# Cross attention's scores of all four units computed at once into four banks, and the router's chain reordered around the count

## The reference

```python
h = h + y @ w_out[layer]                       # after the three mixers
h = h + cross_attention(rms_norm(h, norm_cross[layer]), rms_norm(mem, norm_mem[layer]),
                        x_w_q[layer], x_w_kv[layer], x_q_norm[layer], x_k_norm[layer], x_w_o[layer])
hn = rms_norm(h, norm_ffn[layer])
# layer 0: dense SwiGLU. layer 1: top-2-of-8 experts
...
# cross_attention: 4 heads of 64, 256 memory tokens, QK-norm
s = jnp.einsum('bshd,bmhd->bhsm', q, k).astype(jnp.float32) * HEAD_DIM ** -0.5
p = jax.nn.softmax(s, axis=-1).astype(v.dtype)
o = jnp.einsum('bhsm,bmhd->bshd', p, v).reshape(bsz, seq, X_WIDTH)
...
# moe_swiglu
logits = (x2 @ w_router).astype(jnp.float32)
top_val, top_idx = lax.top_k(logits, TOP_K)
gate = jax.nn.softmax(top_val, axis=-1)
# each token goes through its two experts, weighted by gate
```

## Time and profile before

| | us |
|---|---|
| median of 3 runs | 1373.01 |
| lowest, highest of them | 1373.0, 1373.81 |
| the profiled execution's own time | 1374.09 |
| span of its trace | 1372.3 |
| TensorE busy | 1310.5 (96%) |
| VectorE busy | 636.4 (46%) |
| ScalarE busy | 425.5 (31%) |
| GpSimd busy | 89.8 (7%) |
| granted TensorE clock, mean | 0.976 |
| HBM read | 355.88 MB, 260 GB/s over the span |

### The profile page before, as it was taken

The page is one execution under the profiler, slowest core; times in us unless marked ns, Lnnn a source line. Parts: engine busy times, 40 slices in busy tenths (PEclk is TensorE's granted clock), DMA queues, the critical chain, the costliest instruction groups (busy, mean ns, idle before and its releaser), DMA issues.

```text
span 1372.3 us, 48306 instructions
## 1 busy us (share of the span) xinstructions
PE 1310.5 (96%) x21428; PEld 1079.5 (79%) x21428; DVE 636.4 (46%) x1404; ACT 425.5 (31%) x847; POOL 89.8 (7%) x139
## 2 busy tenths in 40 slices
PE   7998897999999999989789999999999999999998
PEld 5855555777777685554659999999999999999997
DVE  7876313103322237651245555555555555455554
ACT  4425413001002122541313333343333333333332
POOL 0450100000000017000100000000000000000000
PEclk9997899999999999999889999999999999999999
DMA  8530043244241054102649999999999999999990
GB/s 351 211 123 1 1 184 122 90 171 184 104 172 62 34 240 154 63 1 90 248 175 390 426 426 427 426 427 426 426 426 427 427 426 426 427 426 426 426 403 33
DMA packets 32865, 357.68 MB, mean 261 GB/s; under 512 B 3715, under 2 KB 5379, under 8 KB 6700
## 3 DMA queue, kind: packets, MB, share of 16 engines
q1 hardware_dynamic: 30656, 353.78, 62.4%
q10 hardware_dynamic: 2156, 3.18, 0.7%
HBM read 355.88 MB, written 1.06 MB: 260 GB/s over the span
## 4 chain that ended last, share of the span: by engine, by line
PE 88%; DVE 5%; ACT 3%; issue 2%; DMA 1%; POOL 1%; ACTq 0%; POOLq 0%; DVEq 0%
PE bank L2102 29%; PE bank L1556 26%; PE bank L2118 14%; PE bank L2049 6%; PE bank L2164 2%; PE bank L2089 2%; PE bank L1564 1%; PE bank L1829 1%; PE bank L1706 1%; PE bank L1576 1%; PE bank L1894 1%; ACT ring L575 1%; DVE ring L968 1%; PE bank L1650 1%; PE bank L2002 0%
## 5 line engine op out<-in xcount | busy, mean ns | idle before, releaser
L2102 PE MATMUL bank<-R,ring 128*64 128x80 f32 x11264 | 421.7, 233 | 0.7 <-DVEq L950 0.7
L2102 PEld LDWEIGHTS bank<-R,ring 128*64 128x64 f32 x11264 | 403.0, 137 | 8.3 <-issue 8.3
L1556 PE MATMUL bank<-ring 128*128 128x256 f32 (+1 forms) x1408 | 368.4, 421 | 8.6 <-DVE ring L968 4.9
L1556 PEld LDWEIGHTS bank<-ring 128*128 128x128 f32 x1408 | 269.4, 193 | 106.2 <-issue 67.3
L841 ACT ACTIVATE ring<-ring 128x1024 f32<-128x1024 f32 x176 | 186.0, 1057 | 146.7 <-PE bank L2118 146.7
L2118 PE MATMUL bank<-zz,ring 128*64 128x80 f32 x5632 | 224.8, 233 | 0.0
L2118 PEld LDWEIGHTS bank<-zz,ring 128*64 128x64 f32 x5632 | 207.9, 137 | 0.0
L1518 DVE SCALAR_TENSOR_TENSOR zz<-zz,bank 128x80 f32<-128x80 f32 x176 | 41.9, 238 | 198.8 <-PE bank L2102 198.3
L1497 DVE COPY ring<-ring 128x1024 f32<-128x1024 f32 x177 | 121.6, 687 | 1.9 <-DVE R L1487 1.9
L1501 DVE COPY ring<-ring 128x1024 f32<-128x1024 f32 x177 | 121.5, 686 | 0.1
L837 ACT ACTIVATE X<-bank 128x80 f32<-128x80 f32 x176 | 41.7, 237 | 246.1 <-PE bank L2102 246.1
(11 more groups left out here) (299 smaller groups left out, 1029.4 us busy)
## 6 DMA issues: line engine op xcount, KB each, us to landing
ring<-moe_w_dram SPq DMA_DIRECT2D x177, 1536.0 KB, 10.7
ring<-ffn_w_dram SPq DMA_DIRECT2D x11, 3072.0 KB, 10.2
ring<-w_in_dram SPq DMA_DIRECT2D x6, 2048.0 KB, 10.4
ring<-w_out_dram SPq DMA_DIRECT2D x4, 2048.0 KB, 8.5
ring<-w_x_dram SPq DMA_DIRECT2D x2, 3072.0 KB, 10.6
ring<-w_small_dram SPq DMA_DIRECT2D x2, 2896.0 KB, 10.1
ring<-w_in_dram SPq DMA_DIRECT2D x2, 2144.0 KB, 21.0
ring<-bias_rows_dram ACTq DMA_DIRECT2D x1, 1536.0 KB, 11.1
```

Of the source, the lines that this page charges most:

```text
L1556: i = pe.matmul(out_ap, a, b, start=(k == 0), stop=(k == n - 1))
L2102: e = pe.matmul(pb[out_bank][c0:c0 + 64, 0:CAP], half[:, P * k + c0:P * k + c0 + 64], xg[:, k], start=(k == 0), stop=(k == KT - 1), tile_p ...
```

## The change

In cross attention, `xscores(0)` and `xscores(1)` stand next to each other ahead of the loop over the units, and the four units' scores have a bank each (6, 7, 4, 3). `nmx` is used with a place of its own for each unit (`nmx` had four already, for the attention before), so the maxima wait only for the last exponentials of the attention before. In the router, the clearing of `table` and `zeros` stands in front of the wait for the logits, the gate half of the table and the first step of `pos` in front of the wait for the count, and the overflow flag with its signals behind `pick(0)`.

```diff
@@ -44,6 +44,7 @@
 HEADS = [0, 4, 1, 5, 2, 6, 3, 7]
 SLOTS = 4
 BU_BANKS = [3, 4, 7, 1, 3, 4, 7, 3]
+XS_BANKS = [6, 7, 4, 3]
 S5_AT = [dict(bu0=4, bu4=7, bu6=9, ys0=10), dict(bu0=3, bu4=6, bu6=9, ys0=9)]
 UPW, DNW = KT * 2 * 256, 2 * D
 FF_SLOTS = [2, 3, 1, 0, 2, 3, 1, 0, 2, 3, 1]
@@ -213,7 +214,7 @@
             a(f"cross_T{g}_", g % 2)
         a("xq", 2, 2); a("xqT_", 3)
         for u in range(4):
-            a(f"xs{u}_", 6 + u % 2, 0)
+            a(f"xs{u}_", XS_BANKS[u], 0)
             a(f"xpT{u}_", u % 2)
         a("xo0_", 2); a("xo1_", 5); a("xoT", 3)
         for g in range(4):
@@ -570,10 +571,10 @@
                 act.activation(R[:, 0], turn_rows, ACT.Sin,
                                scale=-2 * math.pi, bias=cst[:, C_Q:C_Q + 1]).then_inc(sem["angles_ready"], 1)
 
-            def probs(buf, b, src, scale, to):
+            def probs(buf, b, src, scale, to, m):
 
                 return act.activation(s_of[buf][:, b * src.shape[-1]:(b + 1) * src.shape[-1]], src, ACT.Exp,
-                                      bias=nmx[:, buf, b:b + 1], scale=scale, accum_out=to)
+                                      bias=nmx[:, m, b:b + 1], scale=scale, accum_out=to)
 
             def pt_copy(buf, freed, name, n):
 
@@ -737,7 +738,7 @@
                     if v < 2 * NH:
                         act.wait_ge(sem["max_ready"], u + 1)
                         for b in range(2):
-                            e = probs(at(v), b, s_of[at(v)][:, b * nk:b * nk + nk], 1.0, sums[:, i, b, hh:hh + 1])
+                            e = probs(at(v), b, s_of[at(v)][:, b * nk:b * nk + nk], 1.0, sums[:, i, b, hh:hh + 1], at(v))
                         e.then_inc(sem["probs_ready"], 1)
                     if v == 1:
                         cmp_tanh()
@@ -802,7 +803,7 @@
                         banks.wait(act, f"xpT{k - 2}_{l}" if k >= 2 else f"pT1{NH - 2 + k}_{l}")
                         for b in range(2):
                             e = probs(k % 2, b, ps(f"xs{k}_{l}")[:, 256 * b:256 * b + 256], SCALE,
-                                      sums[:, i, 0, 2 * b + hp:2 * b + hp + 1])
+                                      sums[:, i, 0, 2 * b + hp:2 * b + hp + 1], k)
                         e.then_inc(sem["probs_ready"], 1)
                     if k:
                         pt_copy((k - 1) % 2, u - 2, f"xpT{k - 1}_{l}", 512)
@@ -1395,9 +1396,9 @@
                 for k in range(4):
                     u = 20 * l + 16 + k
                     banks.wait(dve, f"xs{k}_{l}")
-                    dve.wait_ge(sem["probs_ready"], u - 1)
-                    own(dve.tensor_reduce(nmx[:, u % 2], ps(f"xs{k}_{l}")[:].rearrange("p (b s) -> p b s", b=2), AX, ALU.max, negate=True))
-                    dve.tensor_scalar(nmx[:, u % 2], nmx[:, u % 2], SCALE, None, ALU.mult).then_inc(sem["max_ready"], 1)
+                    dve.wait_ge(sem["probs_ready"], 20 * l + 16)
+                    own(dve.tensor_reduce(nmx[:, k], ps(f"xs{k}_{l}")[:].rearrange("p (b s) -> p b s", b=2), AX, ALU.max, negate=True))
+                    dve.tensor_scalar(nmx[:, k], nmx[:, k], SCALE, None, ALU.mult).then_inc(sem["max_ready"], 1)
                 for i in range(NT):
                     dve.wait_ge(sem["probs_ready"], 20 * l + 18 + 2 * i)
                     own(dve.reciprocal(sumc[:, i, 0, 0:4], sums[:, i, 0, 0:4]))
@@ -1432,8 +1433,10 @@
                         dve.scalar_tensor_tensor(hT[:, t % 2], hT[:, 2 + t % 2], 0.5, up[:, 256:512], ALU.mult, ALU.mult).then_inc(sem["gated"], 1)
                     add_in("down")
 
+            own(dve.memset(table, 0.0))
+            own(dve.memset(zeros, 0.0))
+            dve.wait_ge(sem["moe_consts_loaded"], 16)
             banks.wait(dve, "router")
-            dve.wait_ge(sem["moe_consts_loaded"], 16)
             own(dve.tensor_copy(lg, ps("router")[:, 0:16].rearrange("p (i e) -> p i e", i=NT)))
             of_j = lg.unsqueeze(2).to_broadcast([P, NT, E, E])
             of_e = lg.unsqueeze(3).to_broadcast([P, NT, E, E])
@@ -1452,20 +1455,24 @@
             own(dve.tensor_reduce(gsum[:, 0:2], ex, AX, ALU.add))
             own(dve.reciprocal(gsum[:, 0:2], gsum[:, 0:2]))
             own(dve.tensor_tensor(ex, ex, spread(gsum[:, 0:2], [P, NT, E]), ALU.mult))
+            for i in range(NT):
+                own(dve.tensor_copy(table[:, 0:PASSES * E, 2 + i].rearrange("p (q e) -> p q e", e=E),
+                                    ex[:, i].unsqueeze(1).to_broadcast([P, PASSES, E])))
+            own(dve.tensor_scalar(pos, sel, -1e4, 1e4, ALU.mult, ALU.add))
 
             banks.wait(dve, "count")
-            own(dve.tensor_scalar(pos, sel, -1e4, 1e4, ALU.mult, ALU.add))
             own(dve.tensor_tensor(pos, pos, ps("count")[:, 0:16].rearrange("p (i e) -> p i e", i=NT), ALU.add))
-            own(dve.memset(table, 0.0))
+            passes = cste[:, C_PASS - C_MOE:C_PASS - C_MOE + PASSES * E].rearrange("p (q e) -> p q e", e=E)
             for i in range(NT):
-                own(dve.tensor_tensor(table[:, 0:PASSES * E, i].rearrange("p (q e) -> p q e", e=E), pos[:, i].unsqueeze(1).to_broadcast([P, PASSES, E]),
-                                      cste[:, C_PASS - C_MOE:C_PASS - C_MOE + PASSES * E].rearrange("p (q e) -> p q e", e=E), ALU.subtract))
-                own(dve.tensor_copy(table[:, 0:PASSES * E, 2 + i].rearrange("p (q e) -> p q e", e=E), ex[:, i].unsqueeze(1).to_broadcast([P, PASSES, E])))
-            own(dve.tensor_reduce(mx2[:, 2:3], ps("count")[:, 16:24], AX, ALU.max))
-            own(dve.tensor_scalar(flag[:, 0:1], mx2[0:1, 2:3], CAP + 0.5, None, ALU.is_gt))
-            signal(banks.drain("count"))
-            signal(banks.drain("router"))
-            signal(sem["flag_ready"])
+                own(dve.tensor_tensor(table[:, 0:PASSES * E, i].rearrange("p (q e) -> p q e", e=E),
+                                      pos[:, i].unsqueeze(1).to_broadcast([P, PASSES, E]), passes, ALU.subtract))
+
+            def overflow():
+                own(dve.tensor_reduce(mx2[:, 2:3], ps("count")[:, 16:24], AX, ALU.max))
+                own(dve.tensor_scalar(flag[:, 0:1], mx2[0:1, 2:3], CAP + 0.5, None, ALU.is_gt))
+                signal(banks.drain("count"))
+                signal(banks.drain("router"))
+                signal(sem["flag_ready"])
 
             def pick(e, wait_to):
 
@@ -1500,8 +1507,8 @@
                 expert_in(dve, turn, t)
                 dve.tensor_copy(st_value, hs[:, HS_ORDER[t % NHS], 1024:2048]).then_inc(sem["value_staged"], 1)
 
-            dve.memset(zeros, 0.0)
             pick(0, lambda k: dve.wait_ge(sem["e_step"], 1))
+            overflow()
             stage_gate(0, 0)
             for g in range(2):
                 gather_half("", g)
@@ -1993,6 +2000,7 @@
                 drained(f"mkT_{l}")
                 drained(f"xqT_{l}")
                 xscores(0)
+                xscores(1)
                 for k in range(4):
                     u = 20 * l + 16 + k
                     nm = f"xpT{k}_{l}"
@@ -2003,8 +2011,6 @@
                         if l == L - 1 and k == 2 and c == 0:
                             e.then_inc(sem["late0_read"], 1)
                     done(nm, e)
-                    if k == 1:
-                        xscores(1)
                     if k:
                         xvalues(k - 1)
                 xvalues(3)
```

## The result

| | before | changed |
|---|---|---|
| median of 7 runs, us | 1370.88 | 1364.53 |
| lowest, highest | 1369.01, 1373.81 | 1359.97, 1365.95 |
| span of the trace, us | 1372.3 | 1362.9 |
| mean granted clock | 0.976 | 0.981 |

The ratio of changed to before is 0.9946, 95% interval 0.9929 to 0.9963: on 1373 us a gain of 7.4 us, 5.1 to 9.7 (the two medians lie 6.4 us apart). The forecast was 9.5 us of gain and 1363.5 us. Executions of one and the same program differ by 5 to 6 us in this table, and by 7 us in a run further down, so a size under 2 us is read from stages of the traces, not from the medians.

A forecast was written before the change was run, and what follows sets the result against it. TensorE's chain was taken as the bound, with the expert stage a fixed block that starts earlier. Gains of 3.7 + 4.6 + 1.2 = 9.5 us from 1373.0 gave 1363.5 us; own range 1360.8 to 1366, wide range 1360.5 to 1369.3.

The forecast's parts named there:

- wide range: Whole kernel: 1360.5 to 1369.3 us, taking in rivals A and C whole, leaving out B, D and mixtures.
- The wait in layer 0: Layer 0's cross attention: unit 2's exponentials no longer wait for VectorE's maxima, 3.65 us gained, 3.7 with overlap.
- The wait in layer 1: Layer 1's cross attention: exponentials 3.24 us earlier, rest at full clock 1.25 less; 4.5, taken as 4.6.
- The router: Last gate step to table read: memsets, reduction, flag and a pause leave the 2.85 us; 1.2 us gained.
- The cover: Router: warm-up products end at 711.15, gather released at 711.14, so any further gain would meet them.
- The gather's clock: Router's gather, run at 0.50 clock: could gain up to 2.2 us at full clock; taken as 0.
- the fixed block: Expert stage, 81.3 us for each of 8 experts, bound by TensorE: an earlier start ends the kernel equally earlier.
- Rival B: Low clock moves into both output projections, 7.13 us more in each layer: 4.8 us slower, 1377.8; chance 0.03.
- A: Cross attentions: slow clock stays and TensorE bounds the stretch; 1369.3 to 1366 us; chance 0.12.
- C: Router: constants' load lands late, sharing DMA with tiles; 1368.9 us if it took twice as long; chance 0.06.
- D: Expert stage bound by its loads, earlier start given back as tile waits; no change, 1373 us; chance 0.02.
- the weighed rule: Cross attentions: short pauses between matmul groups swing the clock; up to 3.0 us less in layer 0, 2.6 in layer 1.

The follow-up runs named there:

- old_place: Kernel before with only the new banks and `nmx` places, second score products in their old place in both layers; ratio 1.0007 to the kernel before.
- router_only: Kernel before with only the router part of the change, cross attention as before; ratio 0.9991 to the kernel before.
- before_again: The kernel before once more, no edit, for a second trace; 1370.21 us, span 1368.4.
- cross_only: Kernel before with only the cross attention part of the change, router as before; ratio 0.9945 to the kernel before, 7.5 us faster.
- late1: Changed kernel plus one filler product in front of layer 0's feed-forward up products; ratio 0.9933 to the kernel before, median 1362.82 us.
- after_again: The changed kernel once more, no edit; ratio 0.9934 to the kernel before, 9.1 us faster, median 1362.07 us.

## Why the prediction was right, and where its sum was off

**The time.** 1364.5 us against a forecast of 1363.5 looks closer than the working was, and in part this is luck. The forecast took 9.5 us from the 1373.0 of the first three executions; the median of all seven of the kernel before was 1370.9. The base was 2.1 us too high and the gain 2.1 us too large by the ratio (3.1 by the medians), and the two errors cancel. The two traces lie 9.4 us apart, but 3.0 of this are the constants and the gather, which also differ between two executions of the kernel before. The lower end of the wide range, 1360.5, follows from no sum of the working either: its own bounds give 1360.8.

**The wait in layer 0.** Forecast 3.65 to 3.7, measured 3.76 (10.97 or 10.98 us in every trace with the move, 14.72 to 14.75 without). The replay of the old durations behind the copy of unit 0 held to 0.1 us, which is the overlap of ScalarE's instructions (0.48 from start to start for 0.61). Right.

**The wait in layer 1.** Forecast 4.5, taken as 4.6, measured 5.01. The clock stayed at full level, as was taken. The term was 0.4 too small: the first transposes, then also at the full clock, let the copy of unit 0 start earlier, which the working named and counted with 0.1. Unit 2's exponentials started 4.36 us behind the first scores (673.23 - 668.87) for 8.14 before (677.93 - 669.79), 3.8 sooner and not 3.24; the rest took 4.51 for 5.75, as forecast.

**Banks, `nmx` and memsets.** Banks and `nmx` were forecast at 0, and no gain was measured (old_place). The two memsets ran inside VectorE's wait for the constants, as forecast.

**The router.** Forecast 1.2, from the last gate step to the table read 2.85 to 1.6; measured 1.81. The working let the old pause of 0.16 us at the wait for the count go; a pause of 0.26 us stands there in the changed kernel, though the count had ended 0.9 us before (700.45 + 1.25, and 702.58). The cover was misjudged in both directions: the fillers were priced at the 2.66 us of one trace, and took 1.97 at the full clock, where they hold up nothing, and 3.76 at the low one, where they end later than VectorE's matrices. By itself the part gives no measurable gain (router_only, 0.9978 to 1.0003); where the count runs at the full clock it gives 1.0 in its stage.

**The gather's clock.** Taken as 0, seen as 2.0 in the trace, and rightly 0: before_again has it without the change, and the gathers of all traces vary from 2.43 to 4.39 us.

**The missing term.** The step that failed is the sentence that whatever starts the fixed block earlier "ends the kernel earlier by as much", with the next one, that the same holds for layer 0's cross attention. It held for the experts (654.8 and 655.3 us from the first product to the end), and for layer 0's move it did not: the mixers of layer 1 took back 2.5 of 3.76 us by a further low stretch. Rival B had the right kind of mechanism, a low clock brought on by the change, in the wrong place: the output projections ran at full clock in every trace, and the loss came 375 us later. (Against B the prediction said that dense work ended the low stretch of rows 7; that stretch had ended at 682.32, in the last values, 3.5 us in front of the projection.) The terms that are the change's own in the two traces, 3.8 - 2.5 + 5.0 + 1.0, give 7.3 us, and the ratio gives 7.4. That they meet so closely is chance: the interval is 2.3 us wide to either side, and cross_only, without the 1.0, has 7.5. A, C and D did not occur: the clock in both cross attentions was at 1.00, the constants came no later, and each expert kept its 81.2 to 81.3 us. The swing that the weighed rule would have brought did not come there either, though pauses of up to 1.14 us were left between the short groups (214.80 + 2.00 to 217.94).

What stays open: why the third stretch comes with layer 0 3.76 us shorter and not with 0.5 us of it given back, and how the time before the first cross attention (210.8 to 215.3 us in these traces) and the mixers' loss hang together. late1 shows that the place matters; it was tried at one place only.

## What to carry to other kernels

Where an engine works through units in order, look at which unit's first step stands behind another unit's last. Here the work moved up cost nothing, since TensorE was idle while it waited for the first exponentials. A gain in front of stretches where TensorE's work is thin need not be carried down one for one: here 3.76 us became 1.2. Compare stage by stage against a second trace of the unchanged kernel before crediting any stage to an edit. Filler products, meant to keep the clock up, are work in order like any other: here eight records took 1.97 us at the full clock and 3.76 at half, and then the next product waited for them.

## What was not expected of the hardware

- A shift of 3.76 us changed TensorE's clock 375 us later: 0.50 in place of 1.00 over 6.8 us, 2.5 us lost, and one more filler, which shifted the rest by 0.51 us, took it away.
- With layer 0's cross attention as before (five traces), the first low stretch of layer 1's mixers began 358.6 to 358.7 us behind its first scores each time, while those came at 213.4 to 215.2 us. With the move it began at 355.1 to 355.3 in eight traces, and at 353.8 in after_again.
- One filler more in front of the up products gave 2.0 us in its stage; three more in front of the norm's transposes moved the first of them by 0.25 us and delayed nothing behind.
- The same load (the router's constants, 216 KB) took 5.35 us in one execution of the kernel before and 3.9 in the other.
